# A hybrid encoder block on one core: the gate products of a linear recurrence as plain fp32 64x64 blocks, the last two recurrences one group sooner, and three weight pieces split elsewhere or later

## The reference

```
z = rmsnorm(x) @ w_in;  lx, lg, q, k, v = split(z)          # lx, lg: 512 channels each
lx = causal_depthwise_conv(lx, 4 taps)
r, ig = sigmoid(lx_blocks @ w_a + b_a), sigmoid(lx_blocks @ w_i + b_i)   # 8 blocks of 64x64
a = exp(8 * r * log_sigmoid(lambda));  b = sqrt(1 - a*a) * ig * lx
h_t = a_t * h_(t-1) + b_t
y_lru = rmsnorm(h * gelu(lg))
y_att = rmsnorm(windowed attention of q, k, v with sinks and ALiBi)
x = x + concat(y_lru, y_att) @ w_out
x = x + relu(rmsnorm(x) @ w_ff1)**2 @ w_ff2                 # 4096 hidden
x = x + sigmoid(rmsnorm(x) @ w_ple_gate) * (p @ w_ple_proj);  out = rmsnorm(x)
```

## Time and profile before

| | |
|---|---|
| device time, median of 3 runs | 1088.73 us (1082.97, 1088.73, 1088.93) |
| the profiled execution | 1087.07 us, its span 1085.3 us |
| PE busy | 1068.8 us, 98% of the span, 4930 matmuls |
| DVE busy | 688.1 us, 63% |
| ACT busy | 460.3 us, 42% |
| POOL busy | 423.8 us, 39% |
| chain that ended last, by engine | PE 79%, DVE 6%, ACT 2% |

### The profile page before, as it was taken

The page is one execution under the profiler, slowest core; times in us unless marked ns, Lnnn a source line. Parts: engine busy times, 40 slices in busy tenths (PEclk is TensorE's granted clock), DMA queues, the critical chain, the costliest instruction groups (busy, mean ns, idle before and its releaser), DMA issues.

```text
span 1085.3 us, 13820 instructions
## 1 busy us (share of the span) xinstructions
PE 1068.8 (98%) x4930; PEld 877.6 (81%) x4930; DVE 688.1 (63%) x928; ACT 460.3 (42%) x797; POOL 423.8 (39%) x285
## 2 busy tenths in 40 slices
PE   9999999999998999999999999999999999999996
PEld 7888787777876788888888888888888888888896
DVE  7997778878699644544544544544545545697558
ACT  7446745555584322422422422422422422565334
POOL 0121151334127235445445445445445345294221
PEclk9999999999999999999999999999999999999998
DMA  8111102111011112112112112112112111420004
GB/s 330 40 40 39 39 1 88 39 40 40 1 40 39 39 39 77 39 39 77 39 39 77 39 39 77 39 39 77 39 39 76 40 39 73 160 78 1 1 1 156
DMA packets 20162, 61.05 MB, mean 56 GB/s; under 512 B 2080, under 2 KB 4128, under 8 KB 20128
## 3 DMA queue, kind: packets, MB, share of 16 engines
q1 hardware_dynamic: 19440, 59.82, 15.1%
q10 hardware_dynamic: 688, 0.79, 0.2%
HBM read 56.40 MB, written 4.19 MB: 56 GB/s over the span
## 4 chain that ended last, share of the span: by engine, by line
PE 79%; DVE 6%; ACT 2%; issue 1%; DVEq 0%; ACTq 0%
PE bank L576 25%; PE bank L577 25%; PE bank L578 25%; PE bank L683 1%; DVE xT L1781 1%; PE bank L713 1%; PE bank L698 1%; ACT raw L1129 1%; DVE h_lo L1730 1%; PE bank L641 1%; DVE t_lo L1730 1%; DVE xT L1860 1%; DVE r_fin L1362 0%; ACT h_hi L1121 0%; DVE gt L1854 0%
## 5 line engine op out<-in xcount | busy, mean ns | idle before, releaser
L576 PE MATMUL bank<-h_hi,w_hi 128*128 128x512 f32 (+1 forms) x722 | 281.2, 389 | 4.3 <-DVE h_lo L1730 3.7
L577 PE MATMUL bank<-h_lo,w_hi 128*128 128x512 f32 (+1 forms) x722 | 275.2, 381 | 0.0
L578 PE MATMUL bank<-h_hi,w_lo 128*128 128x512 f32 (+1 forms) x722 | 275.1, 381 | 0.0
L1781 DVE TENSOR_TENSOR xT<-bank,xT 128x512 f32<-128x512 f32 x256 | 172.4, 688 | 110.4 <-PE bank L578 110.4
L576 PE MATMUL bank<-u_hi,w_hi 128*128 128x512 f32 x512 | 199.5, 390 | 0.1
L578 PE MATMUL bank<-u_hi,w_lo 128*128 128x512 f32 x512 | 199.2, 389 | 0.0
L577 PE MATMUL bank<-u_lo,w_hi 128*128 128x512 f32 x512 | 199.2, 389 | 0.0
L576 PEld LDWEIGHTS bank<-h_hi,w_hi 128*128 128x128 f32 x722 | 136.1, 188 | 36.3 <-issue 5.2
L577 PEld LDWEIGHTS bank<-h_lo,w_hi 128*128 128x128 f32 x722 | 136.1, 189 | 27.2 <-issue 2.2
L578 PEld LDWEIGHTS bank<-h_hi,w_lo 128*128 128x128 f32 x722 | 136.2, 189 | 26.2
L530 POOL TENSOR_TENSOR w_lo<-w_raw,w_hi 128x1024 fp32r<-128x1024 f32 x30 | 71.9, 2419 | 121.2 <-ACT w_hi L1220 121.2
(11 more groups left out here) (225 smaller groups left out, 1715.1 us busy)
## 6 DMA issues: line engine op xcount, KB each, us to landing
w_raw<-in_w_ff SPq DMA_DIRECT2D x60, 512.0 KB, 3.6
stage<-in_w_in SPq DMA_DIRECT2D x13, 512.0 KB, 6.5
stage<-in_w_out SPq DMA_DIRECT2D x8, 512.0 KB, 4.1
stage<-in_w_ple_gate SPq DMA_DIRECT2D x8, 512.0 KB, 3.6
xT<-in_x SPq DMA_DIRECT2D x7, 512.0 KB, 10.3
stage<-in_w_ff SPq DMA_DIRECT2D x4, 512.0 KB, 3.2
out_x<-xT SPq DMA_DIRECT2D x4, 512.0 KB, 3.0
out_x<-xT SPq DMA_DIRECT2D x6, 256.0 KB, 2.2
```

Of the source, the lines that this page charges most:

```text
L576: pe.matmul(o, whi, hh, start=first, stop=False, skip_group_check=onto)
L577: pe.matmul(o, whi, hl, start=False, stop=False, skip_group_check=onto)
L578: return pe.matmul(o, wlo, hh, start=False, stop=last, skip_group_check=onto)
L1781: dve.tensor_tensor(dst, bank[4 + q % 4][:, :], dst, ALU.add).then_inc(y_added, 1)
```

## The change

Five edits.

1. `gates(j)`: each 128x128 block-diagonal product becomes two plain fp32 matmuls of 64x64 blocks, straight from `yl(j)` and `gate_w`, without high and low parts. The first matrix's blocks go to their own partitions, the second's to the other half of the partitions (`gate_block`), so ACT moves them back with two activations of 64 partitions instead of one of 128. `gx_hi`, `gx_lo`, `gw_hi`, `gw_lo`, what ACT and POOL did for them and their semaphores go.
2. `GATE_AT` becomes `[7, 11, 14, 17]`; gelu of the second pair at g = 16 instead of 17.
3. What follows the recurrences comes one group sooner: `multiply_y(2)`, `(3)` at 19, the squares at 20 and 21, `sum_rows` behind groups 22 and 23, `root`, `invert`, `norm_y` likewise.
4. Before block 0: half 26 is split by POOL instead of DVE, ACT copies half 27 before `root(SS_FFN + 1)`, and that `sum_rows` is two steps later on PE.
5. POOL's `w2_low(1)` waits until `t_low` of t3 is done.

```diff
-GATE_AT = [7, 11, 15, 18]
+GATE_AT = [7, 11, 14, 17]
...
+        def gate_block(i, n):
+            m = n ^ i
+            return slice(m * HD, (m + 1) * HD)
... (POOL)
-            pool.wait_ge(gw_high, 1)
-            pool.tensor_tensor(gw_lo[:, :, :, :], gate_w[:, :, :, :], gw_hi[:, :, :, :], ALU.subtract
-                               ).then_inc(gw_split, 1)
-            for j in range(LT):
-                gate_input_low(j)
             sums(SS_LRU, sq, acc)
             sums(SS_LRU + 1, sq, acc)
...
+            pool.wait_ge(w_split, 2 * FF_FIRST + 2)
+            low(2 * FF_FIRST + 2)
             low(2 * FF_FIRST + 3)
             pool.wait_ge(w_split, 2 * FF_FIRST + 4)
             w1_low(1)
+            pool.wait_ge(t_ready[3], LT)
             w2_low(1)
... (PE)
             def gates(j):
-                pe.wait_ge(gw_split, 1)
+                pe.wait_ge(gatew_in, 16)
+                pe.wait_ge(conv_done, j + 1)
                 for hf in range(2):
-                    pe.wait_ge(gx_low, 2 * j + hf + 1)
                     for i in range(2):
-                        b = 4 + 2 * hf + i
                         if j >= 1:
                             pe.wait_ge(gates_sig, 4 * (j - 1) + 2 * hf + i + 1)
                         else:
                             pe.wait_ge(main_free, 8)
-                        passes(bank[b][:, :], gw_hi[:, i, j, :], gw_lo[:, i, j, :], gx_hi[:, half(hf)],
-                               gx_lo[:, half(hf)], True, True).then_inc(gates_done, 1)
+                    for i in range(2):
+                        for n in range(2):
+                            block = gate_block(0, n)
+                            last = pe.matmul(bank[4 + 2 * hf + i][gate_block(i, n), :], gate_w[block, i, j, block],
+                                             yl(j)[block, half(hf)], start=True, stop=True)
+                        last.then_inc(gates_done, 1)
...
-                if g in (23, 24):
-                    sum_rows(SS_LRU + g - 23, acc, 5)
+                if g in (22, 23):
+                    sum_rows(SS_LRU + g - 22, acc, 5)
...
-                    if hf == 0 and m == 1 and k == 4:
+                    if hf == 0 and m == 1 and k == 6:
                         sum_rows(SS_FFN + 1, acc, 7)
... (ACT)
-            act.activation(gw_hi[:, :, :, :], gate_w[:, :, :, :], ACT.Copy).then_inc(gw_high, 1)
...
-                        act.activation(dst[:, half(hf)], bank[4 + 2 * hf + i][:, :], ACT.Sigmoid,
-                                       bias=bv[:, j:j + 1]).then_inc(gates_sig, 1)
+                        if i == 0:
+                            act.activation(dst[:, half(hf)], bank[4 + 2 * hf][:, :], ACT.Sigmoid,
+                                           bias=bv[:, j:j + 1]).then_inc(gates_sig, 1)
+                        else:
+                            act.activation(dst[gate_block(0, 0), half(hf)], bank[5 + 2 * hf][gate_block(1, 0), :],
+                                           ACT.Sigmoid, bias=bv[gate_block(0, 0), j:j + 1])
+                            act.activation(dst[gate_block(0, 1), half(hf)], bank[5 + 2 * hf][gate_block(1, 1), :],
+                                           ACT.Sigmoid, bias=bv[gate_block(0, 1), j:j + 1]).then_inc(gates_sig, 1)
...
                 if g in GATE_AT:
-                    gate_input_high(GATE_AT.index(g))
                     lru_gates(GATE_AT.index(g))
...
             high(2 * FF_FIRST + 2)
+            high(2 * FF_FIRST + 3)
             root(SS_FFN + 1, 7, r_ffn, D)
-            high(2 * FF_FIRST + 3)
... (DVE)
-                dve.wait_ge(gx_low, 2 * j + 2)
+                dve.wait_ge(gates_done, 4 * j + 4)
...
-                if g == 20:
+                if g == 19:
                     multiply_y(2)
                     multiply_y(3)
+                if g == 20:
                     w_low(2 * 6)
                     w_low(2 * 6 + 1)
...
             for k in range(KD):
                 ffn_low(k, 1)
-            w_low(2 * FF_FIRST + 2)
```

More of the change, by code:

```diff
@@ L116, in build @@
         stage = at("stage", ST, [P, STAGES, HP])
[L118 to L122, removed]
+        gate_w = at("gate_w", Q, [P, 2, LT, P])
         sq = at("sq", T, [P, RING, HALF])
@@ L192, in build @@
         stage_in = [sem(f"stage_in{i}") for i in range(STAGES)]
-        gw_high, gw_split, gx_high, gx_low = (sem(n) for n in ("gw_high", "gw_split", "gx_high", "gx_low"))
         vec_in, gatew_in, bias_in, p_in = sem("vec_in"), sem("gatew_in"), sem("bias_in"), sem("p_in")
@@ L1000, in _ @@
             act.activation(lam[:, 1, :], lam[:, 0, :], ACT.Exp, scale=-1.0).then_inc(lam_exp, 1)
-            act.wait_ge(gatew_in, 16)
-            act.activation(gw_hi[:, :, :, :], gate_w[:, :, :, :], ACT.Copy).then_inc(gw_high, 1)
[L1005 to L1009, removed]
-                for hf in range(2):
-                    act.activation(gx_hi[:, half(hf)], yl(j)[:, half(hf)], ACT.Copy).then_inc(gx_high, 1)
             def lru_gates(j):
@@ L1040, in _ @@
                     act.activation(lru_u[:, :], lru_u[:, :], ACT.Sqrt).then_inc(lru_root, 1)
-                if g in (13, 17):
-                    for j in (2 * (g == 17), 2 * (g == 17) + 1):
+                if g in (13, 16):
+                    for j in (2 * (g == 16), 2 * (g == 16) + 1):
                         act.wait_ge(main_free, 12 if g == 13 else 16)
                         act.activation(gl[:, j, :], gl[:, j, :], ACT.Gelu_apprx_tanh).then_inc(gelu_done, 1)
-                if g in (21, 22):
-                    hf = g - 21
+                if g in (20, 21):
+                    hf = g - 20
                     act.wait_ge(state_done, LT)
@@ L1050, in _ @@
                         square(SQ_BY[SS_LRU + hf] - 4 + j, sq, yl(j)[:, half(hf)])
-                if g in (23, 24):
-                    root(SS_LRU + g - 23, 5, r_lru, LRU)
+                if g in (22, 23):
+                    root(SS_LRU + g - 22, 5, r_lru, LRU)
                 if 22 <= g < 26:
@@ L1565, in _ @@
                     multiply_y(1)
-                if g == 20:
+                if g == 19:
                     multiply_y(2)
                     multiply_y(3)
+                if g == 20:
                     w_low(2 * 6)
                     w_low(2 * 6 + 1)
+                if g == 22:
+                    invert(SS_LRU, r_lru)
                 if g == 23:
-                    invert(SS_LRU, r_lru)
-                if g == 24:
                     norm_y(0)
                     invert(SS_LRU + 1, r_lru)
-                if g == 25:
+                if g == 24:
                     norm_y(1)
```

## The result

The changed kernel takes 1090.47 us (median of 20 runs, 1089.06 to 1091.42), the kernel before 1086.78 us (20 runs, 1081.73 to 1089.36): ratio 1.0037, 95% interval 1.0025 to 1.0049, so 3.7 us or 0.4% slower. The forecast was 1089.4, 2.3 us slower. The profiled execution of the changed kernel took 1090.71 us, span 1088.9. The runs of the kernel before lie in two groups, eight of them near 1082.8 and twelve near 1088.6; experiment 4 shows why. The comparison above takes both together: against the longer group alone the change is 1.8 us slower, against the shorter one 7.6 us.

What follows compares the result with a forecast made beforehand. PE, busy 98% of the span, bounds the kernel, with DVE's and ACT's chain bounding the recurrences. Late sum 2.4 + half clock 1.7 - feed-forward 1.8 = +2.3 us on 1087.07: 1089.4, range 1081 to 1094.

Steps and rivals of the forecast that it cites:

- Gates, four at a time: Gate products on PE: four 64x64 blocks run at once, 2.15 us a gate, 8.6 for all, 4.1 less than before.
- two at a time: Rival, gates on PE: blocks overlap only in pairs, 3.87 us a gate, no wait at the sum, 1088.1 us; chance 0.14.
- one at a time: Rival, gates on PE: blocks do not overlap, 7.3 us a gate, 1101.8 us in all; chance 0.05.
- The recurrences' chain: DVE and ACT through shared buffers, conv(3) costing 4.68 us: decays(3) at 131.6, POOL's additions end at 149.1, 1.1 us gained.
- The wait at the moved sum: PE at the first sum, behind group 22: waits 6.3 us for POOL, 2.4 us late with the restart.
- Half clock: PE behind the wait at the moved sum: 1.7 us lost at 1.2 GHz, between 0 and 3.4.
- Feed forward: Second feed-forward block, edits 4 and 5 together: -4.2 + 0.3 + 2.1 = -1.8 us.
- the 4.3 us that I took: Half 26 on POOL near 307: two blocked h_lo lose 4.3, less 1.2 and about 1: hidden(1) 2.1 us later.
- t3's part: Later w2_low(1): t3's wait and half clock go, PE waits 1.3 us before ff2(1), 4.2 us less.
- The sum's new place gains nothing: Feed-forward's sum_rows two steps later on PE: its 0.4 us wait brings no gain, as ff2(0) waits for DVE anyway.
- POOL stands back for DVE at 306: Rival, half 26 on POOL: the h_lo are not blocked, feed-forward -3.9 us, 1087.3 in all; chance 0.2.
- no wait at the moved sum: Rival: recurrences end a group sooner, PE keeps the gates' 4.1 us, 1079 to 1081 us; chance 0.14.

Runs made afterwards that it cites:

- experiment 4: The kernel before with only w2_low(1) later: 1082.54 us; the kernel before again, unchanged: 1087.72 us; the changed kernel without the later w2_low(1): 1096.75 us.
- experiment 3: The changed kernel with DVE's conv(3) moved behind states(1): 1084.91 us, ratio 0.9968 to the kernel before.
- experiment 2: The changed kernel with the two sums, root, invert and norm_y back at their old groups: 1082.94 us, ratio 0.9965 to the kernel before.
- experiments 1 and 6: The kernel before with the new gates alone: 1085.78 us; the kernel before with the new gates and the later w2_low(1) alone: 1080.04 us.

## Why the prediction was right

- **Gates, four at a time.** Forecast 2.15 us for one, measured 2.10 (2.20 from start to start, less one step of 0.23, and 0.12 more in the two matmuls behind). The sixteen records start in four sets of four, 0.43 to 0.48 us apart. The rivals "two at a time" (3.87) and "one at a time" (7.3) are out. The Trainium skill ("TensorEngine Tiling (Array Packing)", restrictions) says that different row tiles cannot access the same PSUM bank at the same time. This trace does not agree where the tiles write different partitions, as here: the two 64-row blocks of a product write the same bank, and their records start 6 to 7 ns apart.
- **The recurrences' chain.** The mechanism was right, and experiment 3 shows it. What was missed: ACT's six sigmoids follow each other in 0.70 to 0.72 us, those of 128 partitions too, where the four before stepped by 0.57 (so 4.2 us instead of my 3.4), and all of it is 0.7 us late from the input. So POOL ended at 150.5, not at 149.1.
- **The wait at the moved sum.** Forecast 6.3 us, measured 6.09; experiment 2 gives 7.5 us back when only the sum's place and what follows it are undone. PE came to it at 144.3, not 142.85: 0.7 from the input, and 0.8 from a weight piece that stood behind `conv(3)` on DVE. That second item was a term left out: I had followed `conv(3)` into the chain but not into the pieces queued behind it. PE came 1.5 us later than forecast and POOL ended 1.4 us later, so that the length of the wait fits so closely is luck. By the measure of the earlier trace rows PE started the sum 3.6 us late, where I had 2.4.
- **Half clock.** Forecast 1.7 us, measured 2.2, within 0 to 3.4.
- **Feed forward.** Forecast -1.8, measured -2.2 (-0.7 + 3.8 - 5.6 + 0.3), but by larger terms: here the sum is right by luck. The `h_lo` lost the 4.3 us that I took, and DVE came to the relu 3.2 us late by the changed kernel's own shift of 5.9, as 4.3 less 1.2 says. The further 1 us that I took off did not come off: PE saw 3.8, not 2.1. Against that, POOL did not block t4's four `t_lo` after t3's: DVE was ahead and kept going, `hidden(1)` came sooner, and the wait of 1.3 us before `ff2(1)` did not appear, so t3's part was -5.6 and not -4.2. These two errors, 1.7 and 1.4 us, nearly cancel. "The sum's new place gains nothing" was off by 0.7.
- **The rivals.** "POOL stands back for DVE at 306" is out (9.69 us), "no wait at the moved sum" is out (6.09 us).
- **Who keeps whom waiting.** A DVE subtraction that had to wait took 2.8 to 2.9 us instead of 0.7, as long as POOL's own subtraction beside it (2.4 to 2.8). The Trainium skill ("SBUF — State Buffer", on the engine ports) says that whichever of DVE and GpSimd starts first keeps the shared pair for its whole instruction and blocks the other; these lengths agree. It leaves open who comes next when POOL arrives inside a DVE instruction and DVE has another one behind it. In the earlier trace rows POOL got in, in the earlier trace rows it stood back, as I had read it, and in the changed kernel it did both: it got in at 312.00 and stood back at 358.73. So my 4.3 us for the two `h_lo` was right, but nothing in the rows of before could tell it from 0: that rival was refuted by the run, not by the argument. The last section has the cases.
- **Against the median.** The sum was made against an execution with t3's wait in it. In the short runs of the kernel before that wait is absent, and against those the change is 7.6 us slower. The 3.7 us of the comparison thus depend on how many short runs happened to be among the twenty; the profiled executions, of which the one before has that wait, differ by 3.6.

## What to carry to other kernels

A group's worth of earlier work on one engine is only had if the whole chain moves: follow it through its shared buffers, and count every block that an index table carries in front of the chain's next step, with all that is queued behind that block. Making PE's own list shorter in front of a fixed event turns into a wait, and the wait into half clock behind it; put the consumer where its producer is done, not where the table says. Where GpSimd and VectorE both read two SBUF operands, let GpSimd wait in the program until VectorE's urgent operations are done: one semaphore was worth 5 to 6 us here and took the longer group of runs away (1081.9 to 1084.8 instead of 1082 to 1091), a second one 2.9 us.

## What the runs showed of the hardware

- Plain fp32 matmuls of 64x64 blocks ran four at a time in the four quarters of the array, two of them into one PSUM bank at different partitions: 16 records of 512 columns in 1.95 us.
- When POOL's 1024-column subtraction, 2.4 us alone, arrives while DVE runs a row of subtractions of its own, it either gets in at the end of the DVE instruction that is running, and the next two DVE instructions take 2.9 us each, or it stays out for the whole row (7.1 us beside eight of them, from 348.01). It got in at 346.94 and 356.62 (experiment 4) and at 312.00; the next DVE instruction started 0.25, 0.06 and 0.45 us after it. It stayed out at 348.01, where the next DVE instruction had started 0.05 us before it, but also at 358.73 and at 307.54, where it started 0.43 and 0.33 us after it. So a lead over the next DVE instruction does not decide it. The form of the running instruction does not either: `SCALAR_TENSOR_TENSOR` ran at 312.00 and at 307.54, `TENSOR_TENSOR` at 358.73 and at 346.94, the latter in the kernel before:

```profile
345.98 1.28 DVE L1730 TENSOR_TENSOR t_lo<-raw,t_hi 128x512 fp32r<-128x512 f32 x2
```

What does decide it stays open.

- PE's waits of 0.25 us (experiment 2), 0.86 us (experiments 1 and 6) and 1.8 us (at 10 us, experiment 4) left the granted clock at 2.4 GHz; those of 2.45 us (experiment 3), 3.75 us (the kernel before) and 6.1 us (the changed kernel) had 1.2 GHz behind them.
